# Router products from the loaded rows, a fixed first expert pair and early weight loads in a two-block kernel

## The reference, cut to what matters

```python
t = modulate(rmsnorm(x, norm2), sh2, sc2)      # x*rsqrt(mean(x*x)+EPS)*norm2*(1+sc2)+sh2
p_grp = softmax(t @ w_rg + b_rg)               # 4 groups, the best one is taken
logit_exp = einsum('td,gde->tge', t, w_re) + b_re   # 8 experts in each group
# the two best experts of the best group, gates = p_group * normalized p_expert
y[token] = sum over its 2 experts e of gate * (silu(t @ w_eg[e]) * (t @ w_eu[e])) @ w_ed[e]
x = x + g2 * y
x = rmsnorm(x, final_norm)
```

## Time and profile before

| what | us |
|---|---|
| median of 3 runs | 3203.22 |
| lowest and highest | 3197.05, 3217.68 |
| the profiled execution's own time | 3201.59 |
| its span in the profile | 3200.0 |

### The profile page before, as it was taken

One profiled execution on the slowest core, in us unless ns is written; L12 is line 12 of the kernel. 1 busy time (PEld: TensorE's weight loads), 2 busy tenths in 40 slices (PEclk: granted clock), 3 DMA queues, 4 the chain that ended last, 5 costly groups with the idle time before them and its releaser, 6 DMA issues. The chain is left out here.

```text
span 3200.0 us, 35537 instructions
## 1 busy us (share of the span) xinstructions
PE 2692.3 (84%) x13358; PEld 1793.9 (56%) x13358; DVE 1265.3 (40%) x1878; ACT 642.6 (20%) x1025; POOL 235.2 (7%) x246
## 2 busy tenths in 40 slices
PE   4999987877794699999992698897976399999992
PEld 2888866752673345445441587786765245445441
DVE  4666217865525211111115555672443411111115
ACT  3322314541302000000002421243121000000002
POOL 0000000000000100000002121111000000000002
PEclk6999998998896799999996799899998599999996
DMA  6742235779523799999995415443644499999995
GB/s 232 261 149 70 82 111 177 232 253 421 207 86 134 313 407 411 412 409 412 412 406 184 119 47 112 80 124 132 211 168 166 160 406 412 409 407 410 411 406 189
DMA packets 294549, 812.03 MB, mean 254 GB/s; under 512 B 38428, under 2 KB 160824, under 8 KB 232240
## 3 DMA queue, kind: packets, MB, share of 16 engines
q1 hardware_dynamic: 246680, 700.08, 58.6%
q10 hardware_dynamic: 32504, 64.66, 5.6%
q0 software_dynamic: 15264, 45.92, 4.1%
HBM read 692.65 MB, written 117.91 MB: 253 GB/s over the span
## 5 line engine op out<-in xcount | busy, mean ns | idle before, releaser
L628 PE MATMUL m_ps_y<-m_wa,m_hTa 128*128 128x512 f32 x560 | 255.5, 599 | 0.0
L607 PE MATMUL m_ps_ga<-m_wa,m_xTa 128*128 128x512 f32 x560 | 254.2, 608 | 0.0
L617 PE MATMUL m_ps_b<-m_wb,m_xTb 128*64 128x256 f32 x2240 | 249.5, 381 | 0.0
L607 PE MATMUL m_ps_ua<-m_wa,m_xTa 128*128 128x512 f32 x560 | 246.0, 592 | 0.0
L1057 PE MATMUL xp_acc<-xp_xh,xp_wh 128*128 128x512 f32 (+3 forms) x600 | 222.3, 371 | 0.0
L1059 PE MATMUL xp_acc<-xp_xh,xp_wl 128*128 128x512 f32 (+3 forms) x600 | 220.4, 367 | 0.0
L1058 PE MATMUL xp_acc<-xp_xl,xp_wh 128*128 128x512 f32 (+3 forms) x600 | 220.3, 367 | 0.0
L617 PEld LDWEIGHTS m_ps_b<-m_wb,m_xTb 128*64 128x64 f32 x2240 | 157.8, 137 | 102.2 <-issue 26.5
L724 DVE TENSOR_TENSOR m_hida<-m_ps_ua,m_sila 128x512 f32<-128x512 f32 x35 | 24.2, 691 | 471.0 <-PE m_ps_ua L607 471.0
L693 ACT ACT_TABLE_LOAD x35 | 44.9, 1283 | 793.5 <-PE m_ps_ga L607 793.5
L2291 PE MATMUL xq_acc<-xq_xh,xq_wh 128*128 128x512 f32 x448 | 181.5, 405 | 10.4 <-DVE xq_xl L2713 5.3
(11 more groups left out here) (531 smaller groups left out, 4286.5 us busy)
## 6 DMA issues: line engine op xcount, KB each, us to landing
m_wa<-in_w_dram SPq DMA_DIRECT2D x102, 1024.0 KB, 15.1
m_wb<-in_w_dram SPq DMA_DIRECT2D x102, 1024.0 KB, 17.0
m_wa<-in_w_eg_dram SPq DMA_DIRECT2D x36, 1024.0 KB, 15.0
m_wa<-in_w_eu_dram SPq DMA_DIRECT2D x36, 1024.0 KB, 13.2
m_wb<-in_w_eg_dram SPq DMA_DIRECT2D x36, 1024.0 KB, 12.8
m_wb<-in_w_eu_dram SPq DMA_DIRECT2D x36, 1024.0 KB, 16.1
m_wa<-in_w_ed_dram SPq DMA_DIRECT2D x36, 1024.0 KB, 15.6
m_wb<-in_w_ed_dram SPq DMA_DIRECT2D x36, 1024.0 KB, 17.6
```

The lines of the kernel that those rows point to most:

```text
L607: last = nc.tensor.matmul(out[:, :], xT_a[:, j, :], w[:, k, :], start=(j == 0), stop=(j == J - 1))
L617: last = nc.tensor.matmul(ps_b[c * SB:(c + 1) * SB, p // 2, :], xT_b[:, j, :], w[:, k, c * HF:(c + 1) * HF], start=(j == 0), stop=(j == J ...
L628: last = nc.tensor.matmul(ps_y[:, d * NF:(d + 1) * NF], hT_a[:, k, :], w[:, c, d * NF:(d + 1) * NF], start=(k == 0), stop=(k == JF - 1))
```

## The change

The same three blocks remain, with these edits.

1. The router's logits are formed from the loaded rows: PE transposes X itself, as soon as it is loaded, and multiplies it by wrs = wr*(1+sc2)*norm2, with the scale per input channel in a column layout (col). The factor rstd per token and the constant row cb = sh2 @ wr + bias are applied at the end by DVE. A group column block is widened from 4 to 8, so NL = 40 columns instead of 36. xs is still computed and stored, but in a ring of RXS = 4 tiles.
2. srow, nrow and shrow are loaded by SP between the X tiles. ACT issues three small column loads, then wrg, wre and br.
3. DVE makes wrs before srow, so it first waits for wre and POOL's copies.
4. nbig comes from a rounding in place of eight comparisons. Expert 0 always gets big blocks only (at least one) and expert 1 always a small block, so pair 0 is always experts 0 and 1.
5. The weight buffers w_a and w_b, their semaphores and `piece` are made in `moe_phase`. SP issues the twelve weight loads of pair 0 in the router block, behind the last store of xs and ahead of the stores of the tables. The SP loop of the expert block starts at pair 1.
6. The factor g2 moves from the combine block to the two copies out of PSUM in the expert block. g2a and g2b (768 KB together) are loaded by ACT at the start of the expert block; g2row and its load go.

```diff
@@ moe_phase, buffers and SP @@
-            xs = sb2("xs", [P, T, D])
+            RXS = 4
+            xs = sb2("xs", [P, RXS, D])
...
                     for t in range(T):
                         sp.dma_start(X[:, t, :], x_t[t]).then_inc(s_x[t], 16)
+                        if t == 0:
+                            sp.dma_start(srow[:, :], mod[4 * D:5 * D].partition_broadcast(P)).then_inc(s_par, 16)
+                            sp.dma_start(nrow[:, :], norm_w.partition_broadcast(P)).then_inc(s_par, 16)
+                        if t == 1:
+                            sp.dma_start(shrow[:, :], mod[3 * D:4 * D].partition_broadcast(P)).then_inc(s_par, 16)
 
                     for t in range(T):
                         sp.wait_ge(s_xs, t + 1)
-                        sp.dma_start(xr_t[t], xs[:, t, :]).then_inc(s_st, 16)
+                        sp.dma_start(xr_t[t], xs[:, t % RXS, :]).then_inc(s_sr[t % RXS], 16)
+
+                    for w, s_w, ps in ((w_a, s_wa, range(4)), (w_b, s_wb, range(4)), (w_a, s_wa, (4, 5)), (w_b, s_wb, (4, 5))):
+                        for p in ps:
+                            sp.dma_start(w[p][:, :], piece(0 if w is w_a else 1, p)).then_inc(s_w[p], 16)
...
 @@ POOL, behind the two copies into wr @@
+                    pool.wait_ge(s_col, 48)
+                    nc.gpsimd.tensor_copy(shb[:, :, :], bc(col[:, 2, :], P, 2)).then_inc(s_wrc, 1)
...
@@ ACT @@
-                    act.dma_start(srow[:, :], mod[4 * D:5 * D].partition_broadcast(P)).then_inc(s_par, 16)
-                    act.dma_start(nrow[:, :], norm_w.partition_broadcast(P)).then_inc(s_par, 16)
-                    act.dma_start(shrow[:, :], mod[3 * D:4 * D].partition_broadcast(P)).then_inc(s_par, 16)
+                    for c, src in enumerate((mod[4 * D:5 * D], norm_w, mod[3 * D:4 * D])):
+                        act.dma_start(col[:, c, :], src.rearrange("(p j) -> p j", j=J)).then_inc(s_col, 16)
...
+                    for t in range(T):
+                        act.wait_ge(s_tr, t + 1)
                         if t >= 2:
+                            act.wait_ge(s_log, t - 1)
+                        nc.scalar.activation(xT[:, t % 2, :, :], ps_t[:, t % 2, :, :], ACT.Copy).then_inc(s_xT, 1)
+                        if t > 0:
+                            act.wait_ge(s_sq, t)
+                        nc.scalar.activation(junk[:, :], X[:, t, :], ACT.Square,
+                                             accum_out=ss[:, t:t + 1]).then_inc(s_sq, 1)
+                        act.wait_ge(s_var, t + 1)
+                        nc.scalar.activation(rstd[:, t:t + 1], ss[:, t:t + 1], ACT.Sqrt).then_inc(s_sqrt, 1)
...
@@ PE @@
-                            pe.wait_ge(s_xs, t + 1)
+                            pe.wait_ge(s_x[t], 16)
...
-                                last = nc.tensor.transpose(ps_t[:, t % 2, j, :], xs[:, t, j::J], ident[:, :])
+                                last = nc.tensor.transpose(ps_t[:, t % 2, j, :], X[:, t, j::J], ident[:, :])
...
+                            if t == 1:
+                                pe.wait_ge(s_ws, 2)
...
+                        if t == 2:
+                            pe.wait_ge(s_wrc, 5)
+                            for j in range(J):
+                                last = nc.tensor.matmul(ps_k[:, 0:NL], shb[:, j, :], wr[:, j, :], start=(j == 0), stop=(j == J - 1))
+                            last.then_inc(s_k, 1)
...
@@ DVE @@
+                    v.wait_ge(s_col, 48)
+                    nc.vector.scalar_tensor_tensor(out=col[:, 1, :], in0=col[:, 0, :], scalar=1.0, in1=col[:, 1, :],
+                                                   op0=ALU.add, op1=ALU.mult).then_inc(s_ws, 1)
+                    v.wait_ge(s_ws, 1)
+                    v.wait_ge(s_wrc, 4)
+                    nc.vector.tensor_tensor(wrs[:, :, :], wr[:, :, :], bc(col[:, 1, :], NL, 2), ALU.mult).then_inc(s_ws, 1)
                     v.wait_ge(s_par, 48)
...
+                        if t >= RXS:
+                            v.wait_ge(s_sr[t % RXS], 16 * (t // RXS))
...
+                    link(nc.vector.tensor_tensor(cb[:, :], ps_k[:, 0:NL], br[:, :], ALU.add))
                     v.wait_ge(s_log, T)
-                    v.wait_ge(s_br, 32)
-                    nc.vector.tensor_tensor(L[:, :, 0:NG], ps_l[:, :, 0:NG], bc(br[:, 0:NG], T, 1), ALU.add)
-                    link(nc.vector.tensor_tensor(L[:, :, 8:8 + NE], ps_l[:, :, NG:NG + NE],
-                                                 bc(br[:, NG:NG + NE], T, 1), ALU.add))
+                    link(nc.vector.tensor_tensor(L[:, :, :], ps_l[:, :, 0:NL], bc(rstd[:, :], NL, 2), ALU.mult))
+                    link(nc.vector.tensor_tensor(L[:, :, :], L[:, :, :], bc(cb[:, :], T, 1), ALU.add))
...
-                    link(nc.vector.tensor_scalar(nbig[:, :], cnt[:, :], float(SB), None, ALU.is_gt))
-                    for k in range(1, SEQ // P):
-                        link(nc.vector.scalar_tensor_tensor(out=nbig[:, :], in0=cnt[:, :], scalar=float(P * k + SB),
-                                                            in1=nbig[:, :], op0=ALU.is_gt, op1=ALU.add))
+                    nc.vector.tensor_scalar(cntb[:, 0:1], cnt[:, 0:1], float(SB), None, ALU.add)
+                    link(nc.vector.tensor_copy(cntb[:, 1:NE], cnt[:, 1:NE]))
+                    link(nc.vector.tensor_scalar(nbig[:, :], cntb[:, :], 1.0 / P, (P - 1.0 - SB) / P - 0.5 + 0.5 / P, ALU.mult, ALU.add))
+                    link(nc.vector.tensor_scalar(nbig[:, :], nbig[:, :], ROUND, None, ALU.add))
+                    link(nc.vector.tensor_scalar(nbig[:, :], nbig[:, :], -ROUND, None, ALU.add))
+                    link(nc.vector.tensor_scalar(nbig[:, 0:1], nbig[:, 0:1], 1.0, None, ALU.max))
...
+                    link(nc.vector.memset(nsml[:, 1:2], 1.0))
...
@@ combine block @@
-                            link(nc.vector.tensor_tensor(a, a, g2row[:, :], ALU.mult))
...
-                    sp.dma_start(g2row[:, :], mod[5 * D:6 * D].partition_broadcast(P)).then_inc(s_row, 16)
...
@@ expert_pairs @@
-                with sp.Fori(0, n) as i:
+                with sp.Fori(1, n) as i:
...
+                act.dma_start(g2a[:, :], g2.partition_broadcast(P)).then_inc(s_g2, 16)
+                for d in range(2):
+                    act.dma_start(g2b[d * SB:(d + 1) * SB, :], g2[d * NF:(d + 1) * NF].partition_broadcast(SB)).then_inc(s_g2, 16)
...
-                    nc.vector.tensor_copy(y_a[:, :], ps_y[:, :]).then_inc(s_ya, 1)
+                    nc.vector.tensor_tensor(y_a[:, :], ps_y[:, :], g2a[:, :], ALU.mult).then_inc(s_ya, 1)
...
-                    nc.vector.tensor_copy(y_b[:, :], ps_b[:, :, :].rearrange("p a f -> p (a f)")).then_inc(s_yb, 1)
+                    nc.vector.tensor_tensor(y_b[:, :], ps_b[:, :, :].rearrange("p a f -> p (a f)"), g2b[:, :], ALU.mult).then_inc(s_yb, 1)
```

More of the change, by code:

```diff
@@ L68, in moe_phase, with piece @@
         junk = sb("junk", [P, D])
+        WF = J // 2 * NF
+        w_a = [sb(f"wa{p}", [P, WF]) for p in range(6)]
+        w_b = [sb(f"wb{p}", [P, WF]) for p in range(6)]
+        s_wa = [sem(f"wa{p}") for p in range(6)]
+        s_wb = [sem(f"wb{p}") for p in range(6)]
+        g_dram, u_dram = (w.rearrange("e (p j) f -> e p (j f)", j=J) for w in (w_gate, w_up))
+        d_dram = w_down.rearrange("e (h p c) d -> e h p (c d)", h=2, c=2)
+        def piece(e, p):
+            return (g_dram, u_dram)[p // 2][e][:, p % 2 * WF:(p % 2 + 1) * WF] if p < 4 else d_dram[e][p - 4]
         with ExitStack() as c2:
@@ L76, in ps2 @@
                 return c2.enter_context(nc.psum_tensor(f"{tag}_{name}", shape, dt))
-            xs = sb2("xs", [P, T, D])
+            RXS = 4
+            xs = sb2("xs", [P, RXS, D])
             xT = sb2("xT", [P, 2, J, P])
-            wr = sb2("wr", [P, J, NG + NE])
+            NL = 8 + NE
+            wr, wrs = sb2("wr", [P, J, NL]), sb2("wrs", [P, J, NL])
+            col = sb2("col", [P, 3, J])
+            shb = sb2("shb", [P, J, P])
+            cb = sb2("cb", [P, NL])
             wrg, wre = sb2("wrg", [P, J, NG]), sb2("wre", [P, NG, J, EG])
-            br = sb2("br", [P, NG + NE])
+            br = sb2("br", [P, NL])
             nrow = sb2("nrow", [P, D])
@@ L158, in moe_phase @@
             s_st = sem("st")
+            s_sr = [sem(f"sr{r}") for r in range(RXS)]
             with nc.Block() as block:
@@ L173, in _ @@
                     sp.dma_start(slot_tok.rearrange("(a b) o -> a (b o)", b=SB), tab[:, :]).then_inc(s_st, 16)
-                    sp.wait_ge(s_st, 16 * (T + 2))
+                    for r in range(RXS):
+                        sp.wait_ge(s_sr[r], 16 * (T // RXS))
+                    sp.wait_ge(s_st, 32)
                 @block.gpsimd
@@ L271, in _ @@
                             v.wait_ge(s_xm, t)
-                            nc.vector.tensor_tensor(xs[:, t - 1, :], xs[:, t - 1, :], shrow[:, :], ALU.add).then_inc(s_xs, 1)
+                            u = xs[:, (t - 1) % RXS, :]
```

(16 more changed lines are left out.)

46 lines of the change are left out of this document (18 added, 28 removed).

## The result

| | before | after |
|---|---|---|
| median, lowest, highest of 20 runs each | 3214.57, 3195.43, 3218.46 | 3193.30, 3188.79, 3195.93 |
| profiled execution, its span | 3201.59, 3200.0 | 3192.65, 3191.0 |
| mean granted clock of the profiled execution | 0.911 | 0.906 |

The ratio is 0.995, 95% interval 0.9936 to 0.9964: half a per cent faster. 3155 was forecast, with a range of 3139 to 3177, and the result lies 16 us above that range's upper end. The times of before lie in two groups, 6 runs from 3195 to 3203 and 14 from 3209 to 3218 (of the first three, two and one); the profile of before is one of the lower group. Those of after lie within 7 us.

What follows compares the result with a forecast made beforehand. PE was taken to bound the pair loop, so gains had to come from the four chained stages around it: 23.8 us in m1 and 22.8 in m2, together 46.6 off 3201.6, giving 3155 us, range 3139 to 3177.

Steps and rivals of the forecast that it cites:

- router loop: Router stage of each MoE: L ready at 1015.2 against 1017.1, gain 1.9 us, bounds -1 and +8.
- wre: Router weight load: lands at 988.9 by queues alternating one for one, so srow starts at 990.4, 5.1 us later than before.
- rival by the Trainium skill's rule: Router loop: queues alternate by packets, so wre lands early; gain 8.0 instead of 1.9, total 3143 us; chance 0.12.
- wrs: Router loop, DVE's scaled router weights, made ahead of srow: takes 0.5 us.
- hold-up by the eight products of sh2 and wr: Router loop, turn 2: PE's extra products may hold ACT up once, taken as 0.4 us, bounds 0 and 3.1.
- The small chain: Small DVE instructions after the router loop: 1.2 instead of 1.8 us, gain 0.5, off by at most 0.3.
- Weights behind the stores: Pair 0's weights land at A + 35.7 (A: end of last add), tables ready at A + 33.5; loss 0.5, bounds 0 and 7.
- Fetch: POOL's first fetch to PE's first product: 13.1 us; gain 10.9 in m1, 9.9 in m2, bounds 7 and 13.
- rival that the fetch is not DMA's: Fetch of pair 0: gathers are as slow without the weights, so no gain there; total 3176 us; chance 0.10.
- Pair loop: Expert block: copies out of PSUM become products of the same size, cost 0; at most 3.5 us in all if not hidden.
- Combine block: Last stage of each MoE: DVE's turn falls from 5.53 to 4.27 us; gain 11.0, bounds 7 and 11.4.
- One pair more: Rival on the number of pairs: 34.42 us more for each MoE, total 3224 us; chance 0.02.

Runs made afterwards that it cites:

- the mirror: Kernel before, with TensorE waiting for wr ahead of the first products instead of the first transposes, so tiles 0 and 1 are transposed apart; median 3230.4 us, ratio 1.0058.
- e1_hold: Kernel after, with TensorE starting no transpose before wrs is ready, so 16 transposes run back to back; four executions, 3176.3 to 3198.5 us, ratio 0.9894.
- experiment 6: Kernel before, unchanged, profiled twice more to see its upper group of times; 3200.2 us and 3216.3 us.
- e5_warm7: Kernel after, with seven unneeded 512-column products between tile 1's transposes and the wait for wrs; 3160.2, 3161.7, 3161.9 and 3171.5 us, ratio 0.9867.
- e7_late: Kernel after, with pair 0's twelve weight loads issued behind SP's last wait, for the tables, instead of behind the xs stores; median 3238.4 us.
- e10_wide_turns: e8_best with two more 256-column products, never read, behind each tile's products; 3157.4 to 3165.9 us, median 3163.2.
- e8_best: Kernel after, with short loads before long ones, and four wide products plus the sh2 and wr products between tile 0's and tile 1's transposes; ratio 0.9839.
- e2_warm: Kernel after, with four unneeded 512-column products between tile 1's transposes and the wait for wrs; 3174.3 to 3187.1 us, ratio 0.9893.
- e9_before_warm: Kernel before, with fourteen wide products ahead of TensorE's wait for wr; eight of ten executions 3198.4 to 3206.2 us, two at 3218, ratio 0.9991.
- e11_swap: e8_best with the tile products' operands exchanged (wrs loaded, transposed rows run past it), an ACT copy and a transpose back; median 3158.5 us.

## Why the prediction was wrong

**The step that failed** is in the router loop: "PE begins its products at 990.4 at half clock (0.50 in the stages without work) ... the bounds are 0 and the same kind of stall as before, 3.1, and I take 0.4". I took the rise of the clock for granted, and bounded its price by a stall that I had seen in a loop where it did rise. At half clock a turn is PE's, 5.01 us and not 2.66; L came 58.9 us after the load of X, not 41.1. The error is 17.8 us in m1 and 17.0 in m2: 35 of the 38 us by which 3155 was missed. It should have been a rival: "the clock does not rise, turn 5.0 us, 3155 + 2 x 17". The rows for it were there. The earlier trace rows has 0.73 for the stage, a mean of two levels, which asks when and after what it rose; and its 23.37 us of PE fill the loop from PE's start to its end. A turn of PE at full clock takes 2.66 us, as long as a turn of DVE, so there was no slack for a slower one. The change took TensorE's dense start apart (16 transposes in one piece, then products) into two lone tiles 4.7 us apart and products after 6.3 us of waiting. That this start is enough for the loss is shown by the mirror; why the start in one piece then gives the clock only sometimes, and in the changed kernel (e1_hold) less often, stays open.

**The baseline hid a part of it.** The profile of before, with both loops at full clock, is not its usual execution: the median of 20 is 3214.6. Set like against like, by experiment 6: with both loops at half clock 3230.4 before (mirror) and 3193.3 after, 37 us; with both at full clock 3200 and 3161 (e5_warm7), 39 us. By this estimate the change is worth 37 to 39 us (the mirror starts TensorE earlier than before does and e5_warm7 has extra products, so neither pair differs in the change alone), and it loses the clock in both loops always, where before lost it in one loop about half of the time.

**Point by point.**

- wre: I counted 988.9 by turns of one long and one short run, 14.9 us after the first load of X (974.03); POOL's copy starts at 990.87 after its wait for that load, 15.4 us after that of the kernel after (975.52). The trace agrees with one for one, and the rival by the Trainium skill's rule (DMA: Bandwidth & Descriptors, Queues, rings and completion order), about 1 us behind shrow, did not come.
- wrs was mis-sized, 1.21 us and not 0.5, so srow started 17.1 us behind the first load (992.66) instead of 16.4; at the loop's true pace that hardly mattered. POOL's copy of shb (1.03 us from 991.36) runs beside it and ends 0.3 us before it; whether it holds wrs back no run tests.
- The hold-up by the eight products of sh2 and wr was mis-sized as well, and a rise of the clock alone would not have saved the 1.9. In e5_warm7, m1, srow starts 16.4 us behind X, as forecast, and DVE keeps its turn of 2.66 us but for one wait of 1.75, for ACT behind those products, where I took 0.4. L is ready 42.8 us behind X against 43.0, a gain of 0.2 instead of 1.9.
- The small chain: -0.5 as forecast.
- Weights behind the stores: the first table was issued 34.1 us after the end of the last add (33.5 forecast), and the DMA engines were at rest from 1066 on, so the weights had landed 33 us after the add (35.7 forecast). POOL followed the second table in 4.0 us in m1 and 5.8 in m2 (4.1 and 4.0 before), so the loss that I put at 0.5 was none in m1 and 1.7 in m2.
- Fetch: 15.1 and 14.4 us where I had 13.1. By its three terms in m1: 4.5 us to the first gather (I had 3.3, from a wait for the indices of 2.55 that is now 3.73), 5.2 to the second (5.2), 5.4 to the first product (4.6). The first and the last were mis-sized, 1.2 and 0.8 us. The rival that the fetch is not DMA's is out by e7_late.
- Pair loop: 34.4 us a pair, 18 and 17 pairs, no cost.
- Combine block: a turn of 4.27 as forecast, DVE's, so the gathers are no bound; the same in m2. One pair more: no.

**The range.** "Its own range, from the bounds of the terms, is 3143 to 3167" does not follow from these bounds: with each at its bad end m1 gains -1 + 0.2 - 7 + 7 + 7 = 6.2 us, twice that is 3189. The narrower range supposes that the bad ends do not fall together, which the prediction does not say. Nor would the sum of the bounds have been right for the right reason: the router loop's -1 was -15.9, while fetch, small chain and combine block stayed inside their bounds. The result lies within 1% of no change, to which I gave 0.12, but for an unchanged fetch and joint mishaps of two terms, not for the clock.

**What the list of signs said.** "No wait of DVE for the products before L" and its start time were the signs for the router, and the wait of ACT for PE in every turn shows them wrong. The sign for the start of srow, 16 to 17 us after the first load, was just missed at 17.1. The list had no line for the clock.

## What to carry to other kernels

A TensorE that comes out of idleness into short, narrow work may stay at 1.2 GHz for the whole stage, busy without a gap; so read the granted clock by stage, ask what the engine did before it rose, and treat an edit that starts it earlier and in pieces as a possible loss, with the stage at doubled PE times as a rival of its own. Where operands come late, products whose result nobody reads, right up to the first needed one, can be worth more than they cost: here 15 us for each loop. And where the times of a kernel lie in two groups, find out which of them the profile belongs to before any number is subtracted from it.

## What the runs showed of the hardware that I had not expected

- Busy and clocked down together: 40 us of PE with 39.3 to 40.0 us busy at 0.50 in both loops of the kernel after, 36 us in one loop of the kernel before. The Trainium skill (TensorE: Matmul & The Clock Gate, Loop structure matters more than you think) advises to let matmuls follow each other immediately, so that the engine keeps its full clock. These rows show that back-to-back alone did not do it here. Pauses of 1.5 to 2.3 us were followed by the fall within the next transposes (e10_wide_turns, e8_best, e2_warm), and in one loop the clock fell without a pause (e5_warm7).
- The same program reached the full clock in a loop or not from one execution to the next: 12 against 11 of 23 for the kernel before beside e9_before_warm, 1 against 7 and 9 against 4 in two other comparisons, 3 against 1 in e5_warm7. What decides it is not shown by these runs.
- In no execution of the kernels with wide products in each turn (e10_wide_turns, 4) or 128-column products (e11_swap, 6) did a time show a loop at half clock to its end, but one profiled loop of e10_wide_turns did fall, and rose again. Narrow loops that had risen fell for good in three profiled executions (e2_warm and e8_best behind a pause, e5_warm7 without). Whether it is the width was not separated from the longer turn.
- A tile's products of 128 columns on 40 loaded ones and those of 40 columns on 128 loaded ones took almost the same time at full clock, 1.94 us (e11_swap) and 1.88 (e8_best).
